# Three block starts of a hybrid decoder kernel: what the sample stage waits for, which branch the merge takes first, and where three weights are asked for

## The reference, cut to what matters

```python
y = gated_rmsnorm(y.reshape(bsz, L, SSM_D_INNER), z, lp['ssm_norm'])     # 1536 wide
a_out = y @ lp['w_a_proj']
b_out = spatial_gating(u, v, lp['gm_ws'], lp['gm_bs']) @ lp['w_b_proj']  # 512 wide
gates = jax.nn.sigmoid(xn @ lp['w_gate'] + lp['b_gate'])
merged = gates[..., :D_MODEL] * a_out + gates[..., D_MODEL:] * b_out
x = x + merged @ lp['w_out']
x = x + cross_attend(rmsnorm(x, lp['norm_mem']), mem_k, mem_v, lp['w_mem_q'], lp['w_mem_o'])
x = x + hier_moe(...)
```

## Time and profile before

| what | value |
|---|---|
| median of 3 runs | 2320.72 us (2319.5 to 2323.49) |
| the profiled execution's own time | 2315.61 us |
| its span (first to last instruction) | 2313.9 us |
| PE busy | 2042.4 us, 88% |
| DVE busy | 1007.4 us, 44% |
| ACT busy | 777.8 us, 34% |
| POOL busy | 362.0 us, 16% |
| data moved | 324.47 MB, 140 GB/s over the span |

### The profile page before, as it was taken

One profiled execution on the slowest core, in us unless ns is written; L12 is line 12 of the kernel. 1 busy time (PEld: TensorE's weight loads), 2 busy tenths in 40 slices (PEclk: granted clock), 3 DMA queues, 4 the chain that ended last, 5 costly groups with the idle time before them and its releaser, 6 DMA issues. The chain is left out here.

```text
span 2313.9 us, 31029 instructions
## 1 busy us (share of the span) xinstructions
PE 2042.4 (88%) x11366; PEld 1774.3 (77%) x11367; DVE 1007.4 (44%) x1108; ACT 777.8 (34%) x1098; POOL 362.0 (16%) x496
## 2 busy tenths in 40 slices
PE   5999999997999997859988998998797499999991
PEld 4788899997888886549986798776677478887881
DVE  3214255553556654442213411354322554884662
ACT  3232122221334443330002312332202164785662
POOL 1000010001434444401010100000001011222112
PEclk9999999999999998879998999999895599999995
DMA  5211232332333442743327002542107257997895
GB/s 176 80 65 49 63 92 83 91 92 75 110 119 109 122 122 72 215 164 111 120 84 250 19 28 73 177 169 96 69 1 287 91 179 256 313 374 246 275 313 178
DMA packets 241766, 324.47 MB, mean 140 GB/s; under 512 B 14081, under 2 KB 159521, under 8 KB 241633
## 3 DMA queue, kind: packets, MB, share of 16 engines
q1 hardware_dynamic: 206628, 267.60, 34.7%
q0 software_dynamic: 6912, 25.17, 4.4%
q10 hardware_dynamic: 28144, 30.54, 3.7%
HBM read 250.45 MB, written 72.82 MB: 140 GB/s over the span
## 5 line engine op out<-in xcount | busy, mean ns | idle before, releaser
L314 PE MATMUL psum<-hT_high,t_w_high 128*128 128x352 f32 x576 | 187.9, 326 | 5.7 <-DVE t_w_low L910 5.7
L3209 ACT ACTIVATE e_w_high<-big 128x2048 fp32r<-128x2048 f32 x96 | 178.6, 1907 | 35.9 <-PEq L2695 26.3
L316 PE MATMUL psum<-hT_high,t_w_low 128*128 128x352 f32 x576 | 186.5, 324 | 0.0
L315 PE MATMUL psum<-hT_low,t_w_high 128*128 128x352 f32 x576 | 186.5, 324 | 0.0
L3293 DVE TENSOR_TENSOR e_w_low<-big,e_w_high 128x2048 fp32r<-128x2048 f32 x64 | 144.0, 2289 | 40.2 <-ACT e_w_high L3209 39.4
L3152 PE MATMUL psum<-e_w_high,e_xT_high 128*128 128x512 f32 x368 | 148.7, 404 | 6.6 <-DVE e_xT_low L3288 4.3
L3153 PE MATMUL psum<-e_w_low,e_xT_high 128*128 128x512 f32 x368 | 146.5, 398 | 0.0
L3154 PE MATMUL psum<-e_w_high,e_xT_low 128*128 128x512 f32 x368 | 146.5, 398 | 0.0
L314 PE MATMUL psum<-hT_high,s_w_high 128*128 128x352 f32 x384 | 131.6, 343 | 0.0
L315 PE MATMUL psum<-hT_low,s_w_high 128*128 128x352 f32 x384 | 124.3, 324 | 0.0
L316 PE MATMUL psum<-hT_high,s_w_low 128*128 128x352 f32 x384 | 124.2, 323 | 0.0
(11 more groups left out here) (481 smaller groups left out, 4808.1 us busy)
## 6 DMA issues: line engine op xcount, KB each, us to landing
big<-in_w_expert_gate SPq DMA_DIRECT2D x32, 1024.0 KB, 8.3
big<-in_w_expert_up SPq DMA_DIRECT2D x32, 1024.0 KB, 11.0
big<-in_w_expert_down SPq DMA_DIRECT2D x32, 1024.0 KB, 12.7
t_w<-in_w_in SPq DMA_DIRECT2D x24, 512.0 KB, 4.4
x_scr<-t_conv_out ACTq DMA_DIRECT2D x20, 512.0 KB, 4.3
gate_scr<-s_gate_tanh ACTq DMA_DIRECT2D x16, 528.0 KB, 3.4
m_gates<-gate_scr SPq DMA_DIRECT2D x16, 528.0 KB, 5.3
s_w<-in_w_gate SPq DMA_DIRECT2D x16, 512.0 KB, 4.1
```

Source lines behind the costliest of these rows:

```text
L314: nc.tensor.matmul(out, ah, w_h, start=start, stop=False)
L315: nc.tensor.matmul(out, ah, w_l, start=False, stop=False)
L316: return nc.tensor.matmul(out, al, w_h, start=False, stop=stop)
L3209: return nc.scalar.activation(dst, src, ACT.Copy)
```

## The change

It has five parts.

1. At the end of `ssd_sample` SP waits for nothing any more. The semaphores of the stores and of the `yT` loads (now one for each load) belong to a new class `MergeIn`, and ACT waits for them in `merge`, ahead of the first split of y. The stores' ring `q_h_new` now lies at the start of the big region, under the place of `yT_high` and not of `uT_high`.
2. The first weights of the merge are loaded by SP inside `ssd_sample`, behind the z loads.
3. The merge takes the u product first and the y product second, for every f. ACT and DVE split in that order: u weights, 4 tiles of u, y weights, 12 tiles of y.
4. The first half of `w_out` is loaded by SP in the merge, behind the gates of f = 1. `out_query` loads only the merged rows and x at its start.
5. Both halves of `w_mem_o` are loaded by SP at the end of `attention`, behind its last loads, and awaited there. In `w_mem_o` ACT and DVE split row tile 0 first, then the weights, then the other row tiles.

The core of the diff:

```diff
+OUT_W_AT = 212960
+MEM_O_AT = 196576
@@ stage_ssd_sample
+        hnew = g.alias32("q_h_new", [P, OUTS, NB, N], g.big_at)
+        bm_at = g.big_at + OUTS * NB * N * 4
...
+            for q in range(2):
+                merge.load(sp, 0, q)
             for u in range(XF):
                 sp.wait_ge(s_hn, u + 1)
                 sp.dma_start(h_out[u], hnew[:, u % OUTS]).then_inc(s_ho[u % OUTS], 16)
...
-            for i in range(OUTS):
-                sp.wait_ge(s_ho[i], 16 * (XF // OUTS))
-            sp.wait_ge(s_yb, 48)
@@ new
+class MergeIn:
+    KT = XF + GMF
+    KS = (slice(XF, KT), slice(0, XF))
+    def __init__(self, g, at):
+        self.w = g.alias32("m_w", [P, self.KT, P], at)
...
+    def load(self, sp, f, q):
+        sp.dma_start(self.w[:, self.KS[q]], self.src[q][:, :, bass.ds(f * P, P)]).then_inc(self.s_w[q], 16)
@@ stage_merge, SP
+            gates(0)
+            weights(1, 0)
+            weights(1, 1)
+            sp.wait_ge(s_ad, 1)
+            gates(1)
+            query_w(sp, s_qw)
+            with sp.Fori(1, DK // 2) as i:
...
+            for i in range(3):
+                sp.wait_ge(s_ho[i], 16 * (XF // 3))
+            sp.wait_ge(s_qw, 64)
@@ stage_merge, PE
-                ah, al = ((yh, yl), (uh, ul))[q]
+                ah, al = ((uh, ul), (yh, yl))[q]
@@ stage_merge, ACT (DVE in the same order, with low parts)
-            for q in range(2):
-                w_high(0, q)
-            for t in range(KT):
-                src, dst = (g.yT[:, t], yh[:, t]) if t < XF else (g.uT[:, t - XF], uh[:, t - XF])
-                nc.scalar.activation(dst, src, ACT.Copy).then_inc(s_sh, 1)
+            w_high(0, 0)
+            for t in range(GMF):
+                nc.scalar.activation(uh[:, t], g.uT[:, t], ACT.Copy).then_inc(s_sh, 1)
+            w_high(0, 1)
+            for i in range(3):
+                act.wait_ge(s_ho[i], 16 * (XF // 3))
+            for t in range(XF):
+                if t % 4 == 0:
+                    act.wait_ge(s_yb[t // 4], 16)
+                nc.scalar.activation(yh[:, t], g.yT[:, t], ACT.Copy).then_inc(s_sh, 1)
@@ stage_out_query, SP
-            load_w(0, 0)
-            load_act(0)
-            for p in range(1, PW):
-                load_w(0, p)
-            for i in range(1, AP_):
+            for i in range(AP_):
                 load_act(i)
@@ stage_attention, SP
+            for j in range(2):
+                sp.dma_start(mem_o[:, j], wv[:, :, j * BANK:(j + 1) * BANK]).then_inc(s_mo, 16)
+            sp.wait_ge(s_mo, 32)
@@ stage_add_rows, ACT (DVE in the same order)
-            w_high(0)
-            for c in range(NT):
+            high(0)
+            for p in range(PW):
+                w_high(0, p)
+            for c in range(1, NT):
                 high(c)
@@ build
+            def query_w(sp, done):
+                wv = d["w_out"][0].rearrange("(k p) n -> p k n", p=P)
+                for p in range(4):
+                    sp.dma_start(query_raw[:, 2 * p:2 * p + 2, :], wv[:, 2 * p:2 * p + 2, 0:BANK]).then_inc(done, 16)
```

More of the change, by code:

```diff
@@ L1730, in stage_merge @@
         mo = g.sb("m_out", [P, 2, T], ctx=ctx)
-        s_w = [g.sem(f"m_w_loaded{i}") for i in range(2)]
+        s_w, s_yb, s_ho = first.s_w, first.s_yb, first.s_ho
+        s_qw = g.sem("m_query_w_loaded")
         s_gt = g.sem("m_gates_loaded")
@@ L1748, in weights, with gates @@
                 sp.wait_ge(s_wl, f * 2 + q + 1)
-                sp.dma_start(w[:, KS[q]], (wa, wb)[q][:, :, bass.ds(f * P, P)]).then_inc(s_w[q], 16)
-            with sp.Fori(0, DK // 2) as i:
+                first.load(sp, f, q)
+            def gates(f):
+                for q in range(2):
+                    sp.dma_start(gt[:, q, :], g.gate_scr[f + q * DK]).then_inc(s_gt, 16)
+            gates(0)
[5 more added lines that the diff above has]
+            with sp.Fori(1, DK // 2) as i:
                 for s in range(2):
```

150 lines of the change are left out of this document (63 added, 87 removed).

## The result

| | before | after |
|---|---|---|
| median of four runs | 2321.77 us (2319.5 to 2323.49) | 2295.08 us (2291.78 to 2298.13) |
| profiled execution, its span | 2315.61, 2313.9 us | 2298.13, 2296.4 us |
| PE busy | 2042.4 us, 88% | 2046.6 us, 89% |

The ratio is 0.9885, with an interval of 0.9864 to 0.9906. The forecast was 2295.8 us.

The account below looks back on a forecast made before the run. PE (88% busy) was taken to be held up by waits at three block starts. Gains of 12.3 (merge), 1.4 (out_query) and 11.2 (w_mem_o), 24.9 us, off the median 2320.72 gave 2295.8 us, range 2287 to 2306.

Parts of the forecast that it names:

- What bounds the kernel: PE waits 17.0, 19.0 and 15.5 us at the starts of merge, out_query and w_mem_o, behind chains over several engines.
- Merge, 12.3 us forecast: Merge's first output tile: its products end at 1031.6 instead of 1043.9, a gain of 12.3 us; low bound 7.5.
- At 1019.7 PE owes 3 + 72 = 75 matmuls, 11.9: Merge's first output tile: after DVE's last y tile PE has 75 matmuls left, 11.9 us, ending at 1031.6.
- the clock in the merge: Rival: PE's clock stays low at DVE's pace in merge, costing 150 us over the whole block, 2446 us; chance 0.02.
- Later output tiles, "Cost 0": Merge's later tiles: same 144 matmuls, 23 us a tile; splitting y weights lies beside u's matmuls, so cost 0.
- The queue behind `w_out`: Merge: early w_out delays the weights of f = 2, all there by 1049; cost 0, some 5 us of cover.
- If 4 MB moved at 117 GB/s: Rival in merge: w_out and f = 2 weights take 36 us, PE stands about 17 us, 2313 us; chance 0.05.
- out_query, 1.4 us forecast: Start of out_query: merged rows no longer follow a 0.5 MB weight quarter, gain 1.4 us; bounds 0 and 4.3.
- w_mem_o, 11.2 us forecast: Start of w_mem_o: PE begins at 1620.9 instead of 1632.1 and the whole move counts, 11.2 us; bounds 10.0 and 13.1.
- that rival: Rival at w_mem_o: the clock is kept over PE's gap of 4.3 us, 1.9 us less, 2293.9 us; chance 0.09.
- a late start: Merge's low bound: block still begins at 1002.3, gain 7.5 us; as a rival 2300.6 us, chance 0.09.
- one more tile in the way: Low bound of w_mem_o: one more DVE tile before PE's start, gain 10.0 us.

Follow-up runs that it names:

- b_keepwait: Changed kernel, but SP waits again at the end of the sample stage for the states' stores and the yT loads; 2300.88 us, 0.9922 of before.
- k_weights_late: Changed kernel, but the merge's first weights are asked for at its start, ahead of the first gates; 2300.72 us, 0.9916 of before.
- d_wmemo_late: Changed kernel, but w_mem_o is loaded at its own block's start and its weights are split first, as before; 2308.21 us, 0.9948 of before.
- a_all: The changed kernel itself, unedited, compared a second time with the kernel before; 2296.60 us, 0.9898 of before.
- j_wout_double: Changed kernel, but the merge loads w_out a second time, ahead of the weights of f = 2; 2303.68 us, 0.9930 of before.
- c_wout_late: Changed kernel, but the first half of w_out is loaded by out_query, as before; 2296.32 us, 0.9900 of before.
- f_oldsplit: Changed kernel, w_mem_o loaded early too, but its four weight quarters are split ahead of row tile 0; 2297.72 us, 0.9900 of before.
- g_addafter: Changed kernel, but in the merge POOL's add also waits until DVE has split the next y weights; 2295.53 us, 0.9888 of before.
- e_yfirst: Changed kernel, but the merge takes y's product first and u's second, as before; 2297.66 us, 0.9900 of before.

## Why the prediction was right, point by point

**What bounds the kernel**: right. PE's waits at the starts of the blocks were what could go, and behind each stood the chain that was named: b_keepwait gives the end-wait back, k_weights_late and d_wmemo_late the late loads, and each puts its own part of the time back.

**Merge, 12.3 us forecast, 10.9 measured.** The first output tile ended 1044.45 - 997.20 = 47.25 us after the sample stage before and 35.47 after: 11.8. The start came as forecast (gates 0.26 us behind DVE, PE 3.45 behind it; the forecast had 3.2), the end-wait did not reappear, the stores were done, and the y tiles ended at 1022.15, 22.5 behind the sample stage, as forecast (1019.7 - 997.2). For the step "At 1019.7 PE owes 3 + 72 = 75 matmuls, 11.9" PE needed 35.47 - 22.5 = 13.0. Some 0.5 of that excess stood before as well (17.5 counted for 111 matmuls, 1044.45 - 1026.32 = 18.1 measured) and drops out of the difference. The other 0.6 is the clock. In the stretch paced by DVE it fell to the low level at about 1016.7, and the first matmuls behind the stretch still ran at it. The prediction had this as a rival for the whole block ("the clock in the merge", 150 us at the full price) and argued that the clock would stand the pace. It stood it in some executions and not in others. In after, a_all, b_keepwait, k_weights_late and j_wout_double it fell; in c_wout_late, d_wmemo_late, f_oldsplit and g_addafter it did not, and these four have the code of after up to there, its pace, and y tiles done at the same 22.5 us. These are stretches of c_wout_late over its y tiles and behind them, and its first tile's end:

```profile
1005.00:1012.00 7.00, 6.10 (x35) 5.23 (x35) 7.00 (x7) 7.00 (x8) 0.00 (x0) 1.00 0.40 112
1012.00:1018.80 6.80, 4.38 (x18) 2.63 (x18) 6.80 (x7) 2.85 (x4) 0.00 (x0) 1.00 0.01 2
```

```profile
1031.19 1.25 DVE L1862 SCALAR_TENSOR_TENSOR m_gates<-m_gates,psum 128x1056 f32<-128x1056 f32 x1 [10.60 <-PE psum L318]
```

The sample stage ended at 996.33 there, so the tile ends 34.9 us behind it: with the clock kept the gain is 47.25 - 34.87 = 12.4, the 12.3 of the forecast, and where it falls 11.8. The price stays at 0.6 because PE only waits in that stretch and had the full clock again from about 1023.5, 1.3 us behind the last y tile.

**Later output tiles, "Cost 0"**: wrong by 0.9 us. The six distances took 139.23 in place of 138.31. The step looked for who waits for DVE's split of the y weights and found time enough; it took the old 1.76 us for it. In the new order POOL's add starts with that split, and the split takes 3.9 to 3.98. g_addafter, which only moves the add, gets all of it back: counted from one tile's last gated product to the next its seven tiles take 161.38 us, as before, against 162.31. (The 0.2 between its 138.51 and 138.31 lies in where the first of those loads of gates stands, and not in the tiles.) e_yfirst's 138.95 has the split back at 1.76 and another cause, `w_out` ahead of the y weights.

**The queue behind `w_out`**: right in kind. Landing by 49 less 997.2 = 51.8 after the sample stage was forecast and 53.9 seen; some 5 us of cover forecast (4.3 with the splitting taken off), 3.4 seen. j_wout_double shows the wait that comes once it is used up, and e_yfirst that with the old order it would already have cost 0.5. "If 4 MB moved at 117 GB/s" is refuted: the mean of a stretch with idle time was not the queue's speed.

**out_query, 1.4 us forecast, 1.8 measured.** The quarter's transfer ahead of the merged rows was the price taken. SP's own time for issuing it, 0.39 in the earlier trace rows, is the rest: one load fewer stands ahead of the rows at SP too. A loss, which the lower bound did not exclude, did not come.

**w_mem_o, 11.2 us forecast, 10.6 measured.** PE's first matmul moved by 11.1 (15.03 to 3.89), as forecast; PE then ran at the low level for 12 matmuls, where it was 9 before, and three at 0.2 more each are the other 0.5. So the whole move did not count, but this 0.5 is not a fixed price: at this place the twelve kernels that load `w_mem_o` early had 10 to 13 slow matmuls, and the two that load it late 9. The clock was not kept over a gap of 4.3 us (first matmul 0.77, clock 0.50 from 1612.3 to 1616.3), against that rival. `a_w` was asked for at 1584.71 and was there 7 us before the block's end (8 forecast), and attention took no longer for it: from SP's last V load to DVE's last instruction it is 24.14 us before and after.

**The sum.** 24.9 forecast, 23.3 by the touched stretches, 24.6 and 26.7 by the medians. The forecast's high bound of each term was not reached and the low ones (a late start, one more tile in the way) did not come true. Taking the sum off the median and not off the profiled time was the better choice: the profiled execution of before was some 6 us under its median, that of after 3 over, and the untouched stretches of after sum to 5.7 more than those of before, which is just what the spans' 17.5 us lack of 23.3. That the median came within 0.7 us of the forecast is luck in part: the terms missed by 1.4 and 0.6 one way and 0.4 the other, and medians of the same kernel differ by 1.5.

**What was missed** is a further gain. The prediction worked out that "PE owes 3 + 72 = 75 matmuls" at the end of DVE's tiles and took it as given. That debt is a loop order, not a bound, and was worth 6.4 us, or 7.0 where the clock fell.

## What to carry to other kernels

Where a block's start is a chain over several engines, walk it back link by link and price each: here an end-wait, a late load and the order of the splits cost 5.0, 5.8 and 2.1 us one behind the other, and the change without one of the first two left about half of the 16.4 us (8.5 and 9.2, against 3.5). Where a producer paces PE, take the loop order in which PE can use all of a tile as it comes, so that no work is left owing. When a difference of half a microsecond turns up in one execution, look whether the same code shows it in others before giving it to the edit. And when an edit moves an instruction of DVE, look at what POOL runs beside it in the new place, since the old duration may not hold there.

## What the runs showed of the chip that was not expected

- **A paced PE can lose the clock, and need not.** Under three matmuls of 352 columns per 1.18 us the granted clock was 1.00 in the kernel before (1018.5 to 1026.3) and in e_yfirst. In the changed order with the slabs outside it was 1.00 and then 0.50 (from about 1016.7 in the changed kernel itself) in five kernels, and 1.00 until DVE was done in four others, c_wout_late among them. In after, a_all and j_wout_double, which lost it, the clock had come up 6.9 us after the sample stage; in the four that kept it, 7.3 to 7.5. Why the one leads to the other stays open.
- **Restarts are not equally long.** The low level lasted 9 matmuls of 512 columns at w_mem_o before and in d_wmemo_late (after gaps of 15.5 and 15.3 us) and 12 after a gap of 4.3 us in the changed kernel; in the other kernels that load `w_mem_o` early it was 10 to 13. So a short gap did not keep the clock and did not shorten the restart.
- **DVE beside POOL.** A split of 128x1536 took 3.98 us beside POOL's add, 1.76 without it, while the add took about the same in either case (2.47 and 2.45).
- **A small load has a time of its own.** 0.25 MB of weights issued behind a 2 MB `yT` load took 5.9 us to reach ACT in k_weights_late, and the fastest of that kernel's 16 loads of `m_w` took 4.7 us to land, so that little of the 5.9 is owed to the load ahead.
